# Reordering the mixers of a two-block transformer: row inputs first, norms split in two, gate units between branch units

## The reference

```python
def token_mixers(h, ...):
    u = h @ w_in                       # rq rk rv rg sz sxbc sdt gq gk gv gr ga mqk mv mo mi mf mgate
    y_ret = head_rmsnorm(retention_scan(q, k, v, log_gamma)) * silu(rg)
    xbc   = silu(causal_dwconv(sxbc, ssd_conv_w, ssd_conv_b))
    y_ssd = rmsnorm_2((ssd_scan(xs, dt, bh, ch, a) + d * xs) * silu(sz))
    y_gla = head_rmsnorm(gla_scan(q, k, v, log_sigmoid(ga @ w_alpha + b_alpha) / 16)) * silu(gr)
    qk    = silu(causal_dwconv(mqk, ml_conv_w, ml_conv_b))
    y_ml  = head_rmsnorm(mlstm_scan(q, k, v, i_pre, log_f)) * sigmoid(mo)
    gates = sigmoid(mgate)             # (seq, 4, 1024)
    merged = sum(gates * einsum('bsnv,nvd->bsnd', [y_ret, y_ssd, y_gla, y_ml], w_branch), axis=2)
    return merged @ w_out
```

## Time and profile before

| | |
|---|---|
| median of 3 runs | 2475.39 us |
| the profiled execution | 2476.7 us, its span 2474.9 us |
| busy: PE, DVE, ACT | 93%, 71%, 53% of the span |
| mean granted PE clock | 0.969 of full |
| second block, mixers of layer 0 | about 717 to 1072 us of the span |
| mixers of layer 1 | about 1278 to 1635 us |

### The profile page before, as it was taken

How to read it: one execution, slowest core, us unless ns; L and a number is a source line. 1 busy time by engine, 2 the same in 40 slices (tenths; PEclk the granted TensorE clock), 3 DMA queues, 4 the chain that set the end, 5 groups by cost and what they waited for, 6 DMA issues and landing times.

```text
span 2474.9 us, 38140 instructions
## 1 busy us (share of the span) xinstructions
PE 2311.9 (93%) x14926; PEld 1965.3 (79%) x14926; DVE 1753.2 (71%) x2743; ACT 1299.8 (53%) x1888; POOL 18.3 (1%) x37
## 2 busy tenths in 40 slices
PE   8999999999999698799999798789999999999998
PEld 7988799988898687699988687677777777777776
DVE  6556676666785557764356547759889889898896
ACT  5545545455453433352243433347767767777674
POOL 0000000000000000000000000000000000000000
PEclk9999999999999899999999899979999999999998
DMA  6433244443564333264544333339999999999993
GB/s 195 145 122 97 92 137 148 133 142 104 122 181 121 110 112 103 99 201 161 173 136 127 112 103 103 102 137 392 349 346 356 351 347 353 347 359 349 342 358 134
DMA packets 255496, 488.82 MB, mean 198 GB/s; under 512 B 35112, under 2 KB 208072, under 8 KB 221400
## 3 DMA queue, kind: packets, MB, share of 16 engines
q1 hardware_dynamic: 249792, 483.87, 56.2%
q0 software_dynamic: 656, 1.71, 0.2%
q10 hardware_dynamic: 4872, 0.81, 0.2%
HBM read 485.30 MB, written 1.05 MB: 197 GB/s over the span
## 4 chain that ended last, share of the span: by engine, by line
PE 68%; DVE 11%; ACT 4%; issue 2%; DMA 0%; DVEq 0%; ACTq 0%; SPq 0%
PE bank L1108 23%; PE bank L742 20%; PE bank L766 10%; PE bank L581 5%; DVE memr L2069 3%; PE bank L550 3%; ACT memr L1580 1%; PE bank L505 1%; DVE mem_high L2564 1%; PE bank L482 1%; DVE mem_high L2606 1%; PE bank L1136 1%; PE bank L622 1%; DVE mem_high L2610 1%; PE bank L780 1%
## 5 line engine op out<-in xcount | busy, mean ns | idle before, releaser
L1108 PE MATMUL bank<-memr 128*128 128x256 f32 (+6 forms) x7440 | 969.2, 290 | 79.2 <-DVE memr L2069 46.7
L1108 PEld LDWEIGHTS bank<-memr 128*128 128x128 f32 (+3 forms) x7440 | 920.2, 189 | 119.8 <-DVE memr L2069 49.9
L970 DVE TENSOR_TENSOR memr_tail<-mem_tail,memr_ring 128x2048 fp32r<-128x2048 f32 x198 | 448.1, 2284 | 32.9 <-ACT memr_ring L838 31.3
L742 PE MATMUL bank<-memr_ring,memr 128*104 128x512 f32 x1492 | 463.3, 396 | 1.4 <-DVE memr L977 1.4
L2069 DVE TENSOR_TENSOR memr<-mem_low,memr 128x1024 fp32r<-128x1024 f32 (+3 forms) x328 | 388.8, 1203 | 78.7 <-ACT memr L1580 77.9
L838 ACT CAST memr_ring<-mem_tail 128x2048 fp32r<-128x2048 f32 x198 | 375.2, 1914 | 77.3 <-PE bank L742 46.7
L1580 ACT CAST memr<-mem_low 128x1024 fp32r<-128x1024 f32 (+3 forms) x328 | 333.4, 1032 | 142.3 <-PE bank L1108 129.8
L742 PEld LDWEIGHTS bank<-memr_ring,memr 128*104 128x104 f32 x1492 | 251.0, 168 | 93.8 <-issue 1.5
L766 PE MATMUL bank<-memr_ring,memr 128*104 128x512 f32 x752 | 243.5, 402 | 1.0 <-DVE memr L1026 1.0
L742 PE MATMUL bank<-memr_tail,memr 128*104 128x512 f32 x536 | 211.3, 394 | 0.0
L766 PEld LDWEIGHTS bank<-memr_ring,memr 128*104 128x104 f32 x752 | 125.3, 168 | 43.2 <-issue 1.2
(11 more groups left out here) (298 smaller groups left out, 2358.5 us busy)
## 6 DMA issues: line engine op xcount, KB each, us to landing
mem_tail<-in_moe SPq DMA_DIRECT2D x198, 1024.0 KB, 4.9
mem_low<-in_w_in SPq DMA_DIRECT2D x112, 1024.0 KB, 5.2
mem_high<-in_moe SPq DMA_DIRECT2D x33, 1024.0 KB, 4.8
mem_low<-in_moe SPq DMA_DIRECT2D x33, 1024.0 KB, 4.9
mem_high<-in_ffn_w SPq DMA_DIRECT2D x30, 1024.0 KB, 8.4
mem_low<-in_w_branch SPq DMA_DIRECT2D x20, 1024.0 KB, 4.9
mem_low<-in_w_out SPq DMA_DIRECT2D x16, 1024.0 KB, 5.3
mem_low<-in_w_in SPq DMA_DIRECT2D x6, 512.0 KB, 3.8
```

The costliest lines, as they stand in the source:

```text
L742: ins = pe.matmul(ACC[g % 2][0:CAP, :], h_[e % 2][:, kk, :], w_[:, 512 * k:512 * k + 512], start=(kk == 0 and i == 0), stop=(kk == KT - 1 ...
L970: TTn(raw_r[n % RAW], raw[n % RAW], hi_f[n % HI], ALU.subtract).then_inc(family("m_split"), 1)
L1108: ins = pe.matmul(out(bank), lhsT, rhs, start=((k, i) == order[0]), stop=((k, i) == order[-1]))
```

## The change

- Units gz5, ga, gz7, mi and mf come right after gz3, and `al` after the first xbc unit. The logarithms on ACT come after the convolution tanhs of xbc, the row chain on DVE right behind; two pairs of low parts are made inside it.
- Each convolution's tanh and product follow its sum by one and two tiles, instead of ten in a row before the scores. PE waits for tiles 0 to 5 before score step 4 and for the others before step 8.
- One gate unit instead of five before the scores.
- The retention and the ssd mixer (norm sums 0 to 2) are normed in the level stage, the other two (sums 3 to 6) between the first branch units. The roots need `asc` instead of an own place; the high and low parts of the normed mixers get own places (`y2_places`).
- One gate unit instead of five around the norms; eight gate units lie between the units of the first two branches, after j = 1, 3, 5, 7.
- A branch chunk has 512 columns and one tile; eight chunks instead of four.
- `low_with` takes the place of `low_after` throughout, and ACT follows mf and sdt.
- The first branch's products go to `sum2` instead of `sq`.

```diff
@@ 461 @@
-        GATES_BEFORE = (3, 2)
         GATES_LEVEL = (2, 1, 1, 1, 1, 1, 1, 1, 0)
...
+        NORM_SETS = (range(0, 3), range(3, 7))
+        NORMED = ((0, 1), (2, 3))
+        GATED = (1, 3)
...
@@ 1336, PE @@
+                ch = split_chunk(win, l, 2692, 2836)
+                feat3(("gz", l, 5), ch, 0, P, T)
+                feat3(("ga", l), ch, P, 16, T)
+                ch = split_chunk(win, l, 3732, 3868)
+                feat3(("gz", l, 7), ch, 0, P, T)
+                feat3(("mi", l), ch, P, 4, T)
+                feat3(("mf", l), ch, P + 4, 4, T)
                 for j in range(6):
                     if j % 2 == 0:
                         ch = split_chunk(win, l, 1280 + j * P, 1280 + (j + 2) * P + (4 if j == 4 else 0))
                     feat3(("xbc", l, j), ch, j % 2 * P, P, T)
+                    if j == 0:
+                        pe.wait_ge(*evacuated("ga", l))
...
+                        gemm(("al", l), [(par2[0:16, c:c + P], rowa[0:16, :])], lambda b: b[:, 0:T])
...
-                gate_units(GATES_BEFORE[0])
+                gate_units(1)
                 pe.wait_ge(*at("rows_ready", l))
...
-                gate_units(GATES_BEFORE[1])
-                pe.wait_ge(*at("conv_ready", l, 9))
+                def norm_sums(part):
+                    pe.wait_ge(*at("o_squares", l, part))
+                    for i in NORM_SETS[part]:
+                        mat, feature_tiles = NORMS[i]
+                        gemm(("ssm", l, i), [(const(mat), squ[:, t, :]) for t in feature_tiles], lambda b: b[:, 0:T])
+
                 for i in range(12):
-                    g = 12 * l + i
+                    if i in (4, 8):
+                        pe.wait_ge(*at("conv_ready", l, 5 if i == 4 else 9))
...
+                norm_sums(0)
                 for n in range(9):
                     levels2(pe, l, n)
                     gate_units(GATES_LEVEL[n])
...
-                gate_units(2)
-
-                pe.wait_ge(*at("o_squares", l))
-                for k, (mat, feature_tiles) in enumerate(NORMS):
-                    gemm(("ssm", l, k), [(const(mat), squ[:, t, :]) for t in feature_tiles], lambda b: b[:, 0:T])
-                gate_units(3)
+                gate_units(1)
                 for n in range(4):
-                    ch = split_pieces(a["w_branch_2"][l, n], 2, D, (0, 512, D))
                     for j in range(KT):
-                        feat3(("br2", l, n, j), ch, j * P, P, T, slots=(2 * n, 2 * n + 1),
+                        if n == 0 and j == 4:
+                            norm_sums(1)
+                        if j % 4 == 0:
+                            ch = split_pieces(a["w_branch_2"][l, n][:, j * P:(j + 4) * P], 2, 512, (0, 512))
+                        feat3(("br2", l, n, j), ch, j % 4 * P, P, T, slots=(0, 1), src=y2_places[n][1:],
                               key=None if j else ("branch2", l, n))
+                        if n < 2 and j % 4 in GATED:
+                            gate_units(1)
@@ 1849, ACT @@
+                gate2(l, 5)
+                copy_unit(rowa[0:16, :], ("ga", l), slice(0, 16))
+                gate2(l, 7)
+                follow("mf", l)
...
                 for j in range(6):
                     copy_unit(xbc[:, j, 3:T + 3], ("xbc", l, j), slice(0, P))
+                    if j:
+                        conv_tanh(j - 1)
+                conv_tanh(5)
+                follow("sdt", l)
...
+                norm_roots(0)
                 gate_tanh(1)
+                roots_of(0)
                 for n in range(9):
...
+                gate_tanh(1)
+                norm_roots(1)
...
+                high_normed(0)
                 for n in range(4):
                     for j in range(KT):
+                        if n == 0 and j == 4:
+                            roots_of(1)
                         follow("br2", l, n, j)
+                        if n < 2 and j % 4 in GATED:
+                            gate_tanh(1)
+                        if n == 1 and j == 1:
+                            high_normed(1)
@@ 2423, DVE @@
+                    low_with("xbc", l, j)
...
+                    if j >= 2:
+                        conv_silu(l, j - 2)
...
+                low_with("mv", l, 2, 1)
                 scan(rowb[32:36, :], tsc[32:36, 2, 0:T], ALU.add, 32, 36)
...
+                low_with("gz", l, 6)
                 scan(tsc[32:36, 2, 0:T], rows[32:36, :], ALU.max, 32, 36)
...
+                def low_gates(n):
+                    for _ in range(n):
+                        low_with("g2", l, gate_low[0])
+                        gate_low[0] += 1
...
                     pick(n)
+                    if n == 1:
+                        normed(0)
                     low_gates(GATES_LEVEL[n])
...
-                        low_after("br2", l, n, j)
+                        low_with("br2", l, n, j)
+                        if n < 2 and j % 4 in GATED:
+                            low_gates(1)
+                        if n == 0 and j == 6:
+                            normed(1)
+                        if n == 1 and j == 2:
+                            low_normed(1)
```

More of the change, by code:

```diff
@@ L243, in build @@
         cols2 = carve(2, 68)
-        top[0] = at_xbc
-        roots = carve(7, T)
+        top[0] = at_gla
+        sum2 = carve(8, T)
+        y2_places = []
+        for place in (at_xbc, upper):
+            top[0] = place
+            y2_places += [(*high_places(2, T), high_places(2, T)[1]) for _ in range(2)]
+        assert top[0] <= at_xbc
         top[0] = at_xbc
@@ L1873, in gate_tanh, with norm_roots, roots_of @@
                         ahead("g2", l, i)
[L1875 to L1878, removed]
-                    st.settle()
-                    st(A(asc[0:n, dst, 0:T], asc[0:n, dst, 0:T], ACT.Exp, scale=-1.0))
-                st(A(stat[0:4, 1, 15:16], pc(f"a_log{l}", parts=4), ACT.Exp))
-                st.settle()
-                for dst, n in ((0, 36), (1, P)):
-                    st(A(asc[0:n, dst, 0:T], asc[0:n, dst, 0:T], ACT.Ln, bias=1.0), sig("ln2", l, dst))
-                gate_tanh(GATES_BEFORE[0])
-                for j in range(10):
-                    act.wait_ge(*at("conv_sum", l, j))
-                    if j >= 2:
-                        act.wait_ge(*at("conv_ready", l, j - 2))
-                    st(A(asc[:, 2 + j % 2, 0:T], conv[:, j, :], ACT.Tanh, scale=0.5), sig("conv_tanh", l, j))
+                gate_tanh(1)
                 act.wait_ge(*at("rows_ready", l))
                 st(A(rowe[0:4, :], rowb[32:36, :], ACT.Exp, scale=-1.0), sig("rowe_ready", l))
-                gate_tanh(GATES_BEFORE[1])
+                def norm_roots(part):
+                    act.wait_ge(*at("o2_done", l, part))
+                    four = slice(4 * part, 4 * part + 4)
+                    st(A(squ[:, four, :], o2[:, four, :], ACT.Square), sig("o_squares", l, part))
+                def roots_of(part):
+                    first, last = NORM_SETS[part][0], NORM_SETS[part][-1] + 1
+                    for i in range(first, last):
+                        b = full(act, "ssm", l, i)
+                        st(A(asc[:, i - first, 0:T], b[:, 0:T], ACT.Ln, bias=eps[:, 0:1], scale=1.0 / (256 if i == 2 else 64)),
+                           free("ssm", l, i))
+                    st.settle()
+                    these = asc[:, 0:last - first, 0:T]
+                    st(A(these, these, ACT.Exp, scale=-0.5), sig("roots_ready", l, part))
                 for i in range(12):
@@ L1908, in _ @@
                     gate_tanh(GATES_LEVEL[n])
-                act.wait_ge(*at("o2_done", l))
-                st(A(squ, o2, ACT.Square), sig("o_squares", l))
-                gate_tanh(2)
-                for k in range(7):
-                    name = ("ssm", l, k)
-                    b = full(act, *name)
-                    st(A(roots[:, k, :], b[:, 0:T], ACT.Ln, bias=eps[:, 0:1], scale=1.0 / (256 if k == 2 else 64)),
-                       free(*name))
-                st.settle()
-                st(A(roots, roots, ACT.Exp, scale=-0.5), sig("roots_ready", l))
-                gate_tanh(3)
+                gate_tanh(1)
+                norm_roots(1)
                 def up_high(F, m):
@@ L1932, in up_high, with high_normed @@
                     st(cp(high, raw), sig("up_high", F, m))
[L1933 to L1936 removed]
+                def high_normed(part):
+                    for n in NORMED[part]:
+                        act.wait_ge(*at("y2_ready", l, n))
+                        for k in range(2):
+                            st.settle()
+                            cp(y2_places[n][1][:, k, :], zs2[:, 2 * n + k, :]).then_inc(*sig("h_high", ("branch2", l, n), k))
                 def high_merged2(j):
@@ L2425, in _ @@
                     gate2(l, j)
-                    low_after("gz", l, j)
+                    low_with("gz", l, j)
                     if j < 2:
                         rope2(("rk", l, j), ret_k[:, j, :])
-                for j in range(6):
```

(11 more changed lines are left out.)

139 lines of the change are left out of this document (77 added, 62 removed).

## The result

The changed kernel takes 2519.6 us (median of 4 runs, 2517.8 to 2521.0) where the kernel before took 2475.5 beside it: a ratio of 1.0174 [1.0156, 1.0191], 44 us slower. The forecast was 2508, between 2478 and 2532, slower with a chance of 0.79. The direction and the place hold, and the time lies inside the range; but the sum had +33 us for the two layers where the profiled executions have +43.9, so 11 us are missing from it.

What follows compares the result with a forecast made beforehand. PE, busy 93%, was taken as the bound, with DVE pacing the level and branch stages. A layer: −29.7 + 0 + 11.2 − 22.0 + 41.5 + 1.5 + 13.9 = +16.4, two +33: 2508 us, range 2478 to 2532.

Steps and rivals of the forecast that it cites:

- What the branch stage costs: Branch units: ACT and DVE queue for a branch tile's buffer, PE waits 4.0 us before gate 25; +41.5 us a layer.
- 14.4 a group: Branch units: time in us from gate 24's end to gate 26's end, against 8.8 of PE work.
- Projections: Projections to the first scores: 84.1 us against 113.8, −29.7 a layer, of which 11.6 is gate units moved away.
- Rival D: Projections and levels: DVE's queue overrated, listed waits do not come; near 2484 us, counted inside the forecast's 0.63.
- the 2.67: Projections: PE's wait in us for low parts of weights, said to end once ACT follows mf and sdt.
- Levels: Level stage: norm sums, late Exp, first normalisations and `low_with` add 11.2 us a layer; levels alternately 4.4 and 5.2.
- The clock: PE at 1.2 GHz behind waits in projections, levels and branch units: 13.9 us a layer, bounds 0 and 16.
- a wait near 3 us or more costs 1.0 to 2.7: Rule for PE's clock: us lost to slower matmuls behind such a wait, used to size the clock term.
- A: Branch stage: gate units fill PE's gaps, first two branches at PE's pace; +19 instead of +41.5, 2443 us; chance 0.14.
- B: PE's clock: all as forecast, but no wait costs clock; 2480 us; chance 0.13.
- C: First two branches: every matmul of the three groups at 1.2 GHz, +15 us a layer, 2538 us; chance 0.10.
- The table load: ACT's roots, taken twice: two more loads a layer at 1.28 us each, without the skill's drain or shared set.

Runs made afterwards that it cites:

- e1: Changed kernel with ACT's casts guarded by order of units instead of order of chunks; 2490.1 us, ratio 1.0065 to the kernel before.
- e8: Kernel before with one thing of the change alone, ACT following sdt and mf; 2468.3 us, ratio 0.997.
- e7: Changed kernel with the first two mixers multiplied by their roots behind the last level instead of behind level 1; 2513.8 us, ratio 1.0153.
- e3: Changed kernel with low parts of the gate units in scores and levels made with `low_after` again; 2493.8 us, ratio 1.0065.
- e5: Changed kernel with six unread fp32 matmuls before the gate units behind j = 3 and 7 of the first two branches; 2505.2 us, ratio 1.0123.
- e2: Changed kernel with the eight branch-stage gate units in pairs after j = 3 and 7 instead of singly after 1, 3, 5, 7; 2477.5 us, ratio 1.0003.
- e9: First half of the change alone (2435.3 us) plus twelve unread matmuls in its 6.60 us wait before the first branch unit; 2433.9 us, ratio 0.9828.

## Why the prediction was right, and where its sum was short

**What the branch stage costs: right.** The forecast named the buffer, the unit that frees it, the order of the casts and the product queued behind; each time of that walk agrees within 0.2 us, and e1 shows the cause by taking it away. The walk without clock (14.4 a group) also holds: the third group took 17.31 us (1601.88 to 1619.19), and 2.3 of it are the slower gate unit. The rest is small: two branch units take 1.70, not 1.5, and the second wait is 1.83, not 1.6.

**Projections: right.** −28.6 against −27.3. The waits were put at 2.2, 0.9, 1.2, 3.7 and 2.2 us; they are 1.64, 0.74, 1.09, 3.30 and 1.90, in the same places. Rival D, that the walk overrates DVE's queue, fell with them. That the new `follow` removes the cause of the 2.67 is shown by e8.

**Levels: right in sum.** +14.1 against 11.2 and 3.0 of clock. `low_with` was to make levels last 4.4 and 5.2 in turn instead of 4.23; e7, where the products are out of the way, has 5.37, 4.29, 5.36, 4.28 and 5.35 us from level 1 on, and e3 gives 4.8 us in layer 1 for `low_with` in that stage, clock included. What the forecast didn't see is that this reaches past the levels, into the gate unit behind the products and into the scores.

**The clock: the term that was mis-sized.** 13.9 us a layer were set down, with 16 as the upper bound. Against the times at full clock the trace of layer 1 has, in the projections 2.7 (72 matmuls in 11.38 us behind the wait of 3.30), in the scores 1.5 (the first gate unit 4.63; another of 4.63 has its like in the kernel before), in the levels 5.1 (4.63, 5.22, 4.50), behind the products 2.2 (5.25), and in the branch stage about 12.5 (gate units of 3.36, 5.49, 4.64, 5.22 and 5.49 make 8.9 more than five of 3.07, two pairs of branch units of 2.86 and 2.43 make 1.9, norm sums and the third branch's first units 1.7). The last two branch units and the output units behind them add 3.1:
```profile
1650.87 2.97 PE L1116 MATMUL bank<-memr_tail,memr 128*128 128x256 f32 x12 [2.62 <-DVE mem_high L2663]
1653.64 24.80 PE L1116 MATMUL bank<-memr 128*128 128x256 f32 x192
```
The kernel before has 1.67 for such 12, and 21.57 for 180; the granted clock is 0.50 from 1650.87 to 1653.64 and 0.53 to 1657.00. Together 27.1 us, which is 13.2 more than set down. The kernel before has half clock too, so PE's busy time in layer 1 grew by less, 16.1 us (289.6 against 273.5).

The other terms came out 4.8 lower, and the difference is the 8.4 us that layer 1 cost beyond the forecast. But the 27.1 are busy time, not all of it time lost. In the branch stage much of it is on the path: e5 gives 8.6 us back there in layer 1. In the levels only a part is: e2, with the same code up to the first product, has 4.0 us less in these three gate units and a stage only 2.1 shorter (50.7 against 52.8).

The step that failed is the rule that only "a wait near 3 us or more costs 1.0 to 2.7". In the levels gate units of 4.63 and 4.50 stand behind waits of 2.23 and 2.20 us, and the scores' first one of 4.63 behind 1.90. And the products' gate unit, the scores and the output units had no clock term at all.

That the total came out within 11 us owes something to layer 0: it cost 2.5 us more than the 16.4 set down, while layer 1, which was walked through, cost 8.4 more.

**Rivals.** A (the gate units fill the branch stage, decided by a wait under 1 us): the wait is 4.11. Another placement goes a little over half the way: e2 has all eight gate units in the branch stage and is 42 us faster, but at 2477.5 still 34 us above A's 2443. B (the clock stays up) fell to the granted clock of 0.69 to 0.87 in the last three stages, and to e5, where filled waits alone give 14.4 us. C (half clock through the first branches) fell to the gate units of 3.03 to 3.07 in the same groups.

**The table load.** The row with the Ln's load is 1.28 us here too, the Ln follows at 1494.66, 0.09 us behind the load, and the Exp has a load of its own. So the 1.28 stand. The extra drain that the Trainium skill, "ScalarE: Activation LUTs", section "What ACT_TABLE_LOAD costs", adds to each switch isn't seen, and neither is the set shared by Ln and Exp that its section on table sets has.

**What stays open.** Why the wait before the second level (2.23 and 2.24 us) is followed by a gate unit of 4.63 in the changed kernel and of 3.11 in e2 and e7, though it costs nothing there. What the chunks of 512 columns, the split norms and `low_with` cost each in the branch stage. And why layer 0 gained 4.5 us more than layer 1 ahead of the products.

## What to carry to other kernels

When two streams of tiles share two buffers and one engine refills them in a fixed order, walk through one period with the unit that frees each buffer: the helper stands at a buffer whose last user comes later than the bank it should empty, and all users of a chunk first and then the others took 42 us less than the two in turn. A step that asks for work only just begun (`low_with`) is a wait in an in-order queue; ask for the work of the step before (26 us here), above all where that engine is the bound. And of a change that gains in one stage and fills gaps in another, build the first half alone: here it was worth −40 us, and the rest took 84 back.

## What the hardware showed that was not expected

- The lower clock takes more than the waits suggest: about 27 us of PE's busy time in layer 1, in a kernel whose PE is busy 93% before and after. Behind waits of 2.2 us in the levels 24 matmuls took 4.63 and 4.50 us in the changed kernel, and 3.11 each behind the same waits in e2, so the last wait alone doesn't tell it. Behind the first of them the next level came 5.37 us later in both: what half clock takes, a wait for DVE can give back.
- Matmuls whose result nobody reads, put into a wait, keep the clock up: six fp32 matmuls, 12 in the trace's count and 2.75 us, in front of each of eight gate units gave 14.4 us back (e5), net of a gate unit elsewhere that fell to 4.60. Where DVE sets the pace they gave nothing that can be measured (e9).
- Removing a stall can bring half clock to the next one: in e8 the wait of 2.27 us stayed as it was, and the 48 matmuls behind it went from 5.89 to 7.44 us.
